# An expert-gather kernel followed by a two-layer block: the block's first layer in two token halves, the first beside the second half of the gather

## What is computed

```python
idx = jnp.take_along_axis(cand_idx..., pos, axis=-1)      # 8 heads x 16 per token
ue = jnp.take(u_tab, idx, axis=0)
ve = jnp.take(v_tab, idx, axis=0)
act = jax.nn.gelu(jnp.einsum('thkd,td->thk', ue, t))
return jnp.einsum('thk,thkd->td', g * act, ve)
...
x = x + g2 * peer(h2, ...)        # then rmsnorm(x, final_g)
```

```python
kv = mem @ mem_w_kv
for i in range(2):
    y = mlstm_mixer(x, ...) if i == 0 else pool_mixer(x, ...)
    x = layer_norm(ALPHA * x + y, ...)
    x = layer_norm(ALPHA * x + memory_cross_attn(x, mem_k, mem_v, ...), ...)
    x = layer_norm(ALPHA * x + sq_relu_mlp(x, ...), ...)
```

## Time and profile before

| | us |
|---|---|
| median of 3 runs | 3493.74 |
| lowest, highest | 3491.20, 3499.36 |
| the profiled execution | 3496.58 |
| its span, first to last instruction | 3494.8 |

### The profile page before, as it was taken

How to read it: one execution, slowest core, us unless ns; L and a number is a source line. 1 busy time by engine, 2 the same in 40 slices (tenths; PEclk the granted TensorE clock), 3 DMA queues, 4 the chain that set the end, 5 groups by cost and what they waited for, 6 DMA issues and landing times. The chain is left out here.

```text
span 3494.8 us, 33128 instructions
## 1 busy us (share of the span) xinstructions
PE 2945.1 (84%) x10628; PEld 1938.5 (55%) x10628; DVE 2257.4 (65%) x3761; ACT 926.1 (26%) x2350; POOL 1856.1 (53%) x1099
## 2 busy tenths in 40 slices
PE   6889898877778877888877779979899975889998
PEld 5667676632333323444433267657678864667886
DVE  7793464376666667776766583675855577586556
ACT  2115402233433333333333322221200012220001
POOL 2544375464444444666554264254577763557874
PEclk9899899999999999999999989989999987999998
DMA  5531122699999999999999811011122220112221
GB/s 216 185 113 55 43 79 73 241 421 419 413 418 412 412 422 409 391 389 399 390 422 418 341 66 55 31 60 61 60 90 96 91 72 12 61 60 93 94 96 55
DMA packets 126107, 719.21 MB, mean 206 GB/s; under 512 B 13200, under 2 KB 16400, under 8 KB 60176
## 3 DMA queue, kind: packets, MB, share of 16 engines
q0 software_dynamic: 73728, 536.90, 37.4%
q1 hardware_dynamic: 46560, 161.18, 13.4%
q10 hardware_dynamic: 5680, 19.40, 1.5%
HBM read 715.33 MB, written 2.10 MB: 205 GB/s over the span
## 5 line engine op out<-in xcount | busy, mean ns | idle before, releaser
L712 PE MATMUL psum<-slots,acc 128*128 128x512 f32 x2048 | 1016.2, 643 | 267.9 <-ACT acc L1167 267.4
L398 POOL TENSOR_TENSOR whi<-w,zeros 128x1024 fp32r<-128x1024 f32 x277 | 548.1, 1979 | 883.1 <-PE psum L469 566.4
L428 POOL DMA_INDIRECT slots<-in_experts,consts x512 | 564.1, 1102 | 675.0 <-PE psum L712 603.5
L1719 DVE SCALAR_TENSOR_TENSOR arena<-slots,work 128x1024 f32<-128x1024 f32 x512 | 663.2, 1295 | 400.1 <-DMA slots<-in_experts,consts 383.1
L712 PEld LDWEIGHTS psum<-slots,acc 128*128 128x128 f32 x2048 | 393.7, 202 | 868.5 <-ACT acc L1167 462.3
L401 POOL TENSOR_TENSOR wlo<-w,whi 128x1024 fp32r<-128x1024 f32 x277 | 718.2, 2593 | 21.7
L467 PE MATMUL psum<-xhi,whi 128*128 128x512 f32 x1104 | 451.5, 409 | 8.7 <-POOL wlo L401 5.6
L468 PE MATMUL psum<-xlo,whi 128*128 128x512 f32 x1104 | 441.8, 400 | 0.0
L469 PE MATMUL psum<-xhi,wlo 128*128 128x512 f32 x1104 | 440.5, 399 | 0.0
L467 PE MATMUL psum<-yhi,whi 128*128 128x512 f32 (+1 forms) x736 | 300.1, 408 | 49.9 <-POOL ylo L453 20.7
L468 PE MATMUL psum<-ylo,whi 128*128 128x512 f32 (+1 forms) x736 | 296.2, 402 | 0.0
(11 more groups left out here) (266 smaller groups left out, 3671.3 us busy)
## 6 DMA issues: line engine op xcount, KB each, us to landing
w<-in_stream SPq DMA_DIRECT2D x277, 512.0 KB
arena<-in_wmod SPq DMA_DIRECT2D x4, 2048.0 KB, 17.8
arena<-in_wmod ACTq DMA_DIRECT2D x8, 1024.0 KB, 6.1
acc<-in_wmod ACTq DMA_DIRECT2D x8, 1024.0 KB, 8.3
slots<-in_experts,consts POOLq DMA_INDIRECT x512
xres<-in_xT SPq DMA_DIRECT2D x1, 2048.0 KB, 15.3
outT<-xres SPq DMA_DIRECT2D x8, 256.0 KB, 2.0
consts<-in_consts SPq DMA_DIRECT2D x1, 1056.0 KB, 5.2
```

The source lines that it names most:

```text
L398: pool.tensor_tensor(hi, w32[:, s, :], zeros[:, :].broadcast_to((P, 1024)), ALU.add)\
L428: pool.indirect_dma_start(out=slots[p % SLOTS], out_offset=None, in_=a["experts"], in_offset=bass.IndirectOffsetOnAxis(ap=indices[:, p:p + ...
L712: mm = pe.matmul(bank(4 + half), diag[:, p % 2, :], v[:, half * T:(half + 1) * T], start=(c == 0), stop=(c == PICKS - 1))
L1719: dve.scalar_tensor_tensor(dot_out, slots[p % SLOTS][:, 0:D], 1.0, tokens[:, p // PICKS, :], ALU.mult, ALU.mult, accum_out=inner[:, c:c + ...
```

## The change

Three things are done at once.

1. The gather is cut at pick 256 (EARLY). Picks 0 to 255 run as before, but with six slots instead of eight, with the memory's sixteen tiles from pick 96 on, and with all sixteen units of the search for experts done by then, one for every 16 picks. DVE's dot product now writes over the row that it has read.
2. Layer 0 runs twice over 256 tokens (H), `lstm0` to `mlp0` and `lstm1` to `mlp1` with matmuls of 128x256. Its 113 weight tiles are therefore loaded, split and used twice (390 tiles in the stream for 277). The second half attends to the keys and values of both.
3. In the first half every engine's program has the picks 256 to 511 among its layer work: two for each weight tile, more at a few places, by a table (`pick_ends`). Half buffers leave five slots for these picks (0 to 3, and 6 in `acc`). POOL gathers four picks ahead and splits three tiles ahead.

Layer 1 is unchanged but for names and indices. The core of the diff:

```diff
-SLOTS = 8
-MEM_AT, MEM_EVERY = 288, 8
+EARLY = NPICKS // 2
+MEM_AT, MEM_EVERY = 96, 8
+H = T // 2
+    for half in range(2):
+        section(f"lstm{half}", [1] * 17)
+        section(f"core{half}", [-1 - half, 1, 1, -3] * 4)
+        section(f"lout{half}", [1] * 8)
+        section(f"xq{half}", [1] * 4 + ([-1] + [1] * 2) * 2 + [-1, -1])
+        section(f"xo{half}", [1] * 8)
+        section(f"mlp{half}", [1] * 64)
...
+def pick_ends():
+
+    first = SECTIONS["lstm0"][0]
+    ends, end = {first - 1: (EARLY, EARLY + 10)}, EARLY + 10
+    more = {first + 16: 4, SECTIONS["xq0"][0] + 5: 2, SECTIONS["xq0"][0] + 7: 2}
+    gaps = {SECTIONS["lout0"][0] + 7: 6, SECTIONS["xo0"][0] + 7: 6}
+    groups = {first: 2, SECTIONS["xq0"][0]: 4, SECTIONS["mlp0"][0]: 4}
+    for n in range(first, SECTIONS["lstm1"][0]):
+        end += sum(2 * (n == g + k - 1) * k - 2 * (g <= n < g + k) for g, k in groups.items())
+        end += 2 + more.get(n, 0)
+        ends[n] = (end, end + gaps.get(n, 0))
+        end = ends[n][1]
...
+    slots = [(4, 5, 0, 1, 2, 3)[p % 6] if p < EARLY else (2, 3, 6, 0, 1)[(p - EARLY) % 5] for p in range(NPICKS)]
...
+            n0, n1, p = first_tile("lstm0"), first_tile("lstm1"), EARLY + 4
+            for m in range(n0 - 1, n1):
+                if m + 3 >= n0 + RING:
+                    next_tile(m + 3)
+                while p < min(NPICKS, picks_by(m, True) + 4):
+                    gather(p)
+                    p += 1
+            split_tiles(n1 + 3, mixed)
...
+            def half_linear(n, o, XH=XHH, XL=XLH):
+                linear(n, o, XH, XL, H)
+                sum_picks(n)
...
-            for p in range(NPICKS):
+            for p in range(EARLY):
                 expert_dot(p)
-                u = p // UNIT + 1
+                u = p // 16 + 1
```

More of the change, by code:

```diff
@@ new lines, in _ @@
+            sum_picks(first_tile("lstm0") - 1)
+            for half in range(2):
+                ni = 3 + 4 * half
+                norm_sums(ni, H, w=wh)
+                norm_spread(ni, H)
+                half_lstm_in(half)
+                half_lstm_core(half)
+                norm_sums(ni + 1, H, mean=True, w=wh)
+                norm_spread(ni + 1, H)
+                half_cross(half)
+                norm_sums(ni + 2, H, mean=True, w=wh)
+                norm_spread(ni + 2, H)
+                half_mlp(half)
+                norm_sums(ni + 3, H, mean=True, w=wh)
+                norm_spread(ni + 3, H)
@@ L994, in root, with affine @@
                 act.activation(r, r, ACT.Sqrt).then_inc(sem("root_ready"), 1)
-            def affine(ni, scale, bias, dst, cols=T, last=None, between=None, order=range(KB)):
+            def affine(ni, scale, bias, dst, cols=T, last=None, between=None, order=range(KB), w=work):
                 for i, k in enumerate(order):
@@ new lines, in half_copy, with half_read, ready, half_post_norm @@
+            def half_copy(dst, o, cols=H, func=ACT.Copy, **more):
+                src = half_product(o)
+                free(act.activation(dst, src[:, 0:cols], func, **more), o)
+            def half_read(o, width=1):
+                def ready(k):
+                    weigh_picks(LAST_TILE[o + k // width])
+                    wait_read(act, o + k // width)
+                return ready
+            def half_post_norm(half, ni, j, ready, n):
+                cols = slice(H * half, H * half + H)
+                squares(ni, lambda k: acc_h[:, k, :], H, ready=ready, w=wh)
+                weigh_picks(n, True)
+                root(ni, H)
+                affine(ni, lambda k: vec("ln_g", 8 * j + k), lambda k: vec("ln_b", 8 * j + k),
+                       lambda k: xres[:, k, cols], H, order=MIX_ORDER if ni == 10 else range(KB), w=wh)
@@ new lines, in half_post_norm @@
+            def half_post_norm(half, ni, n):
+                cols = slice(H * half, H * half + H)
+                dot_gap(n)
+                statistics(ni, LN_EPS, H, mean=True)
+                order = MIX_ORDER if ni == 10 else range(KB)
+                scale = normalise(ni, lambda k: acc_h[:, order[k], :], H, mean=True, w=wh)
+                if ni == 10:
+                    pool_mixer(scale)
+                elif ni == 6:
+                    for k in range(KB):
+                        scale(k)
+                else:
+                    norm_out(ni, scale, lambda k: xres[:, k, cols], lambda k: xhi_h[:, k, :], lambda k: xlo_h[:, k, :])
@@ L1901, in pool_mixer @@
                         scale(2 * n + 3)
+            for half in range(2):
+                half_lstm_in(half)
+                half_lstm_core(half)
+                half_cross(half)
+                half_mlp(half)
             def post_norm(ni, last=False):
                 statistics(ni, LN_EPS, mean=True)
-                scale = normalise(ni, lambda k: acc[:, MIX_ORDER[k] if ni == 6 else k, :], mean=True)
-                if ni == 6:
-                    pool_mixer(scale)
-                elif last:
+                scale = normalise(ni, lambda k: acc[:, k, :], mean=True)
+                if last:
                     for k in range(KB):
```

1218 lines of the change are left out of this document (770 added, 448 removed).

## The result

The changed kernel takes 3871.76 us (median of 4 runs, 3866.54 to 3885.37), the kernel before 3492.47: a ratio of 1.109, 95% interval 1.1064 to 1.1117, 379 us slower. The direction was forecast, the size was not: 3691 us, and no more than 3850. The profiled execution took 3866.5 us, its span 3864.7.

A forecast was written before the change was run, and what follows sets the result against it. POOL's work, splits and gathers, was to bound the joined stretch and the second half alone. First 640 us, B, C, D and layer 1: 640 + 730 + 1029 + 670 + 623 = 3692 us of span, median 3691, range 3540 to 3850.

The forecast's parts named there:

- C: Joined stretch, layer 0's first half with picks 256 to 511, 113 tiles: bound by POOL's work, 1029 us.
- D: Layer 0's second half alone, 113 tiles loaded and split anew: 670 us, ends 600 and 750.
- the meetings with DVE's dots: In the joined stretch, a dot that meets a split costs POOL 0.82 us; one of two does, 0.8 a tile.
- The rule of the Trainium skill: VectorE with two SBUF inputs and GpSimd reading SBUF exclude each other: 8.4 us a tile, sum 46 us higher.
- Stage B: The first 256 picks, with the search for experts twice as dense and six slots: 730 us.
- six slots hold less against a burst than eight; 0 to 60, I take 15, near the low end: First 256 picks: bursts of the search cost between nothing and some 60 us with six slots; 15 taken.
- Stage C ahead of the MLP: Joined stretch before the first half's MLP, 49 tiles: 505 us by the forecast's terms.
- 2.80 + 4.37 + 0.8 = 8.0 us a tile: Joined stretch, POOL per tile: two gathers, a tile's two splits, meetings with dots; 904 us for 113 tiles.
- for norms, taps and heads I take 60 us: Joined stretch: waits where DVE and ACT make the chain in norms, LSTM taps and core's heads, 60 us.
- POOL's lower passes, with which the forecast wanted PE's idle time to end: Sign of being right, from about 1370 to 2400 us: PE's idle time ends with POOL's `wlo`.
- the waits as holes that picks would fill: Joined stretch: picks fill part of the waits in the chains of DVE and ACT, taken at 60 us.
- The second rival: Five slots are too few, the slot's round sets the joined stretch: 1178 us at 23 a round, 3871 in all; chance 0.20.

The follow-up runs named there:

- a_act_hi: The changed kernel with the upper pass of each weight tile moved from POOL to ACT, from the first half's fifth tile on: 3653.24 us, ratio 1.0454.
- a_dot_thin: The changed kernel with dots over 256 of 1024 columns from the sixth pick of the second half on: 3770.98 us.
- b_dense: The kernel before with eight slots and the whole search for experts beside the first 256 picks: 3490.31 us, ratio 0.9985.
- b_six: The kernel before with six slots for the picks' rows instead of eight, all else as it was: 3604.14 us, ratio 1.0318.
- a_fine: The changed kernel with the search cut into 24 pieces of some 0.5 us behind the picks, in place of four longer ones: 3809.38 us.
- a_all_thin: a_act_hi plus, from the second half's sixth pick on, half-long rows, dots over 256 columns, matmuls over 128, a copy for the Gelu: 3430.57 us.
- a_four: The changed kernel with four slots in place of five for the second half's picks: 3935.59 us.
- a_pe_thin: The changed kernel with a pick's two matmuls over 128 of 512 columns from the sixth pick of the second half on: 3852.89 us.
- a_no_table: The changed kernel with a plain copy on ACT for the Gelu from the sixth pick of the second half on: 3881.04 us.

## Why the prediction was right and wrong

**The direction and its reason held.** Halving the tokens doubles POOL's splits, and the MLPs of C and D are POOL's: 523 us for 524, 8.17 us a tile for 8.0, and in D's MLP POOL was busy 304 of 325 us. a_act_hi shows it by giving POOL 1.90 us less a tile: 79 and 101 us came back in the two MLPs, and 38 in D ahead of its MLP, where POOL is busy for 62% and only part of the chain.

Two of the right numbers have luck in them. D's 671 us for 670 is a sum of two errors: POOL's work in it was 493 us [the windows above] for 537, its idle time 178 for 133. And the meetings with DVE's dots, a guess from two rows, were 0.8 us a tile for the splits, beside gathers at 1.10. a_dot_thin took 0.95 away, 0.41 of it on the splits and 0.54 on the gathers. Against the passes alone and the gathers' 1.10, the means of C are 0.45 + 2.25 x 0.1 = 0.67 us a tile, an estimate, so 0.8 was somewhat high for what it stood for. The rule of the Trainium skill that was weighed there (SBUF — State Buffer, "Who interferes with whom") would have made it 1.23 and the MLP 8.4 us a tile; 8.17 lies between the two, and the 0.67 is farther from the rule than from the row.

**Stage B, the step "six slots hold less against a burst than eight; 0 to 60, I take 15, near the low end".** It measured 90. The mechanism was named, its size was not: the reason given for the low end, that the DMA stood at 1.01 through the same bursts with eight slots, is no evidence for six. b_dense shows that eight slots hide nearly all of even the dense bursts, and b_six that with six 7.3 us of a search's 13.1 come through. The bound itself was too low too: 15 searches of 13.1 us could have cost anything up to 196. A number that says "no loss with eight" can bound nothing below eight; what would have is how near a round was to breaking. Part of that was in the trace: at 2.516 us a pick six slots leave 15.1 us for gather, landing, dot, weight and matmul in a row, and pieces of up to 5.5 us come on top. How long a round takes without queueing was not measured. a_fine gave back 62 of the 90 us.

**Stage C ahead of the MLP, the steps "2.80 + 4.37 + 0.8 = 8.0 us a tile" and "for norms, taps and heads I take 60 us".** Both fail there. It is not 8.0 us a tile plus 60 for 49 tiles, but 343 us, which is what the same part takes by itself, plus 118 picks at 2.02. That POOL's busy time does not set it is shown by a_act_hi (6 us for 105 taken from POOL), with the new wait on ACT as the reservation made there: over D's 304.5 us in that run the picks are 2.30 each and not 2.02. From 1370 to 2400 us PE's loads waited 187 us for ACT's weights of picks and 3 for POOL's lower passes, with which the forecast wanted PE's idle time to end. The forecast took the waits as holes that picks would fill. a_all_thin says that they were not: what was made smaller at one link of a pick came off the sum whatever stood at the others. Which wait makes up the half that is left stays open. The second rival had the place and the sort of mechanism right (a pick waits in order behind tiles on DVE, ACT and PE), and even the time, 3871. But that is luck: it put all of C under the slots, 1178 us where 1126 were measured, D at 700 for 671, and took B at 730 for 805, and the errors cancel. As it stood, a fixed round, it is refuted by a_four, where the round fell from 24.6 to 21.2 us with one slot less.

**What the change costs in the large.** A half takes 343 + 325 = 668 us by itself, two take 1336, where the whole layer took 873: 463 us more. In return 244 picks in C cost (1119 - 668)/244 = 1.85 us each and not 2.516: 162 us less. With stage B's 90 on top that is 391, against 370 between the two spans of 3864.7 and 3494.8 us; the 21 between the two this rough account doesn't place.

## What to carry over

Before work is cut in halves so that one half can lie under something else, price the half by itself: here it took 77% of the whole, because each weight tile is loaded and split again, and no overlap could pay that back. A ring of buffers is sized against the longest piece of other work on any engine of the ring, not against the mean; where buffers can't be had, cut that piece smaller (62 and 92 us here). And where work that crosses five engines in order is threaded through a chain that does the same, don't count the chain's idle time as free: here the times added. And when a pass is moved to another engine, look for the new wait: POOL's 219 us for ACT in a_act_hi are what an otherwise good move (219 us less in all) left behind.

## What the runs showed of the hardware

- ACT rounds a 128x1024 fp32 tile to fp32r in 1.04 us (1.038 to 1.066 over 222 passes in a_act_hi), where POOL takes 1.90 to 2.08 with a pass by `tensor_tensor`.
- A gather issued by POOL lasts 0.94 us by itself, 0.96 on the mean beside dots of 256 columns (a_dot_thin) and 1.20 beside dots of 1024; in a_act_hi 1.37 (266.3 us for 194).
- Taking 111 us of busy time from PE in a part where it waits on others gave a lower granted clock, 0.73 for 0.87, and 20 us (a_pe_thin).
- Taking away thirty-one table loads of 1.28 us on ACT, which was busy 215 of 581 us, gained 7.5 us, no more than the noise (a_no_table).
- A dot of 128x1024 that starts beside a split pass of POOL lasts 3.12 us for 1.23.
